# Token rows fetched by index and transposed, in place of gather products, in a four-layer mixture-of-experts step

## What is computed

```python
def moe(h, router_w, router_b, wg, wu, wd):
    x = h.reshape(B * T, D)                                   # 256 x 1024
    scores = jax.nn.sigmoid((x @ router_w).astype(jnp.float32))
    sel = scores + router_b.astype(jnp.float32)
    ...                                                       # best group of 4 experts, its best two
    w = w / w.sum(axis=-1, keepdims=True)
    combine = jnp.einsum('nk,nke->ne', w, jax.nn.one_hot(idx, N_EXPERTS, dtype=jnp.float32))
    hid = jax.nn.silu(jnp.einsum('nd,edf->nef', x, wg)) * jnp.einsum('nd,edf->nef', x, wu)
    y = jnp.einsum('nef,efd->nd', hid * combine[..., None].astype(hid.dtype), wd)
    return y.reshape(B, T, D)
```

## Time and profile before

| | |
|---|---|
| median of three runs | 1986.24 us (1983.18 to 1988.86) |
| the profiled execution | 1988.12 us, span 1986.3 us |
| TensorE busy (MATMUL records) | 1845.2 us, 93% |
| VectorE, ScalarE, GpSimd busy | 482.3, 385.8, 12.3 us |
| moved by DMA | 593.34 MB, mean 299 GB/s |
| granted TensorE clock, mean | 0.96 |

### The profile page before, as it was taken

The page is one execution under the profiler, slowest core; times in us unless marked ns, Lnnn a source line. Parts: engine busy times, 40 slices in busy tenths (PEclk is TensorE's granted clock), DMA queues, the critical chain, the costliest instruction groups (busy, mean ns, idle before and its releaser), DMA issues.

```text
span 1986.3 us, 22833 instructions
## 1 busy us (share of the span) xinstructions
PE 1845.2 (93%) x9280; PEld 1115.4 (56%) x9280; DVE 482.3 (24%) x1240; ACT 385.8 (19%) x801; POOL 12.3 (1%) x24
## 2 busy tenths in 40 slices
PE   4988999999999969999999997999999969999986
PEld 2656644545735858745445565844554748444543
DVE  0132511104300341411112434321112143311102
ACT  1132200003102660200002223200002142000002
POOL 1000000000000000000000000000000000000000
PEclk8998999999998988999999998999999989999988
DMA  9992599996997332579998884559999445599960
GB/s 328 350 401 80 212 397 427 428 419 242 356 359 259 117 122 91 215 311 428 428 427 311 321 292 170 215 216 425 428 429 401 140 193 211 233 424 429 427 265 22
DMA packets 126142, 593.34 MB, mean 299 GB/s; under 512 B 8008, under 2 KB 15312, under 8 KB 101088
## 3 DMA queue, kind: packets, MB, share of 16 engines
q1 hardware_dynamic: 115728, 585.12, 74.0%
q10 hardware_dynamic: 9840, 6.51, 1.1%
q0 software_dynamic: 480, 0.39, 0.1%
HBM read 587.28 MB, written 4.73 MB: 298 GB/s over the span
## 4 chain that ended last, share of the span: by engine, by line
PE 70%; DMA 18%; DVE 5%; ACT 4%; issue 2%; ACTq 1%; SPq 0%; DVEq 0%
PE PS L865 23%; PE PS L1358 18%; DMA ring<-in_moe_wu 16%; PE PS L1337 7%; PE PS L1369 7%; PE PS L894 3%; PE PS L914 2%; PE PS L1317 1%; DMA ring<-in_attn_w_qkv 1%; DMA ring<-in_w_mod 1%; PE PS L932 1%; ACT arena L594 1%; DVE RS L1495 1%; PE PS L1254 1%; PE PS L1322 1%
## 5 line engine op out<-in xcount | busy, mean ns | idle before, releaser
L1358 PE MATMUL PS<-ring,arena 128*64 128x512 f32 x1312 | 353.0, 595 | 4.8 <-DMA ring<-in_moe_wu 3.1
L1337 PE MATMUL PS<-arena 128*128 128x128 f32 (+3 forms) x1584 | 252.1, 317 | 10.8 <-ACT arena L800 4.4
L1337 PEld LDWEIGHTS PS<-arena 128*128 128x128 f32 (+1 forms) x1584 | 222.7, 195 | 52.5 <-issue 25.0
L800 ACT ACTIVATE arena<-PS 128x512 f32<-128x512 f32 (+2 forms) x131 | 71.3, 545 | 873.2 <-PE PS L1369 359.3
L865 PE MATMUL PS<-HS,ring 128*128 128x256 f32 x1024 | 233.8, 386 | 3.5 <-DVE HS L1565 1.6
L1369 PE MATMUL PS<-ring,arena 128*64 128x512 f32 x1024 | 226.8, 595 | 3.4 <-DVE arena L1822 3.4
L865 PEld LDWEIGHTS PS<-HS,ring 128*128 128x128 f32 x1024 | 194.8, 193 | 39.0 <-issue 10.0
L1358 PEld LDWEIGHTS PS<-ring,arena 128*64 128x64 f32 x1312 | 114.4, 137 | 159.6 <-issue 158.4
L1841 DVE TENSOR_TENSOR arena<-arena,PS 128x512 f32<-128x512 f32 x32 | 33.5, 1047 | 556.6 <-PE PS L1358 556.6
L865 PE MATMUL PS<-arena,ring 128*128 128x256 f32 (+1 forms) x672 | 147.6, 381 | 2.7 <-ACT arena L608 1.5
L1369 PEld LDWEIGHTS PS<-ring,arena 128*64 128x64 f32 x1024 | 70.7, 137 | 135.7 <-issue 127.9
(11 more groups left out here) (309 smaller groups left out, 1393.8 us busy)
## 6 DMA issues: line engine op xcount, KB each, us to landing
ring<-in_moe_wd SPq DMA_DIRECT2D x64, 2048.0 KB, 12.2
ring<-in_moe_wu SPq DMA_DIRECT2D x49, 2048.0 KB, 22.1
ring<-in_w_mod SPq DMA_DIRECT2D x48, 2048.0 KB, 16.1
ring<-in_moe_wg SPq DMA_DIRECT2D x33, 2048.0 KB, 19.7
arena<-in_moe_wg SPq DMA_DIRECT2D x32, 2048.0 KB, 20.8
HS<-in_moe_wu SPq DMA_DIRECT2D x16, 2048.0 KB, 28.4
ring<-in_mlstm_w_in SPq DMA_DIRECT2D x12, 2048.0 KB, 8.8
ring<-in_attn_w_qkv SPq DMA_DIRECT2D x6, 2048.0 KB, 20.1
```

The costliest lines, as they stand in the source:

```text
L800: A(dst, src, func).then_inc(S(sem), 1)
L1337: return mm(out, rows, onehot, start=first, stop=final, skip_group_check=True)
L1358: ins = mm(PS[64 * e:64 * e + 64, b, :], XG[:, k, 64 * e:64 * e + 64], w[:, k], start=(k == 0), stop=(k == KD - 1))
```

## The change

For pairs 1 to 7 the gather products are taken out. Token rows are written to memory once a layer, and for each pair GpSimd fetches the rows that its 128 slots need, by a list of 128 indices, into one of the two halves of `HT`; TensorE then turns them with eight transposes (`turn_x`). Pair 0 keeps its products. In detail:

- ScalarE, after each half of `HT` is copied, issues a DMA of it to `HR` in memory (2 x 512 KB).
- VectorE makes `OH`, for both halves of the tokens and pairs 1 to 7 at once: 1 where a token's rank is the slot (two comparisons of 128 x 896). `PB` is made for pair 0 alone, so later pairs have four comparisons in place of eight.
- TensorE's `slot_id`, between the two up groups of pair 0, multiplies each `OH` block by the token's number less 300 (one column): 14 products. VectorE adds 300 and turns the result into whole numbers, `IDX`. An unused slot gets 300, beyond the 256 rows; such an index is skipped and the slot keeps what it held (its weight is 0).
- GpSimd waits for `IDX`, for `HR` and for the half of `HT` to be free, and issues one indirect DMA a pair. Pair p's waits until pair p - 2 is turned (pairs 1 and 2: pair 0's gather).
- ScalarE's first SiLU waits for `slot_id`, since `OH` lies where `SG`, `HID` and `HTS` lie.
- SP, after the last weights of a layer, reads both halves of `HT` back from `HR` (2 x 512 KB), since the overflow step still gathers by products; ScalarE and VectorE wait for it before the next mixer, and TensorE before an overflow step.
- The many semaphores of the overflow step are folded into three. Its work is the same.

```diff
+        IDX = sb("IDX", [P, NPAIR], I32)
+        HR = nc.dram_tensor("token_rows", (N2, D), F32).ap()
+        OH = ar(4096, 2, NPAIR, 2, SLOTS)
...
                 n += 3 * NE
+                sp.wait_ge(S("gather"), 2 * NPAIR * (l + 1))
+                for s in range(2):
+                    sp.dma_start(HT[:, s], HR[P * s:P * s + P]).then_inc(S("back"), 16)
...
+            def rows(l):
+
+                pool.wait_ge(S("idx"), l + 1)
+                pool.wait_ge(S("rows"), 32 * (l + 1))
+                for p in range(1, NPAIR):
+                    pool.wait_ge(S("gather"), 2 * NPAIR * l + 2 * max(p - 1, 1))
+                    pool.indirect_dma_start(HT[:, p % 2], None, HR, bass.IndirectOffsetOnAxis(IDX[:, p:p + 1], 0),
+                                            bounds_check=N2 - 1, oob_is_err=False).then_inc(S(f"slot_rows{p % 2}"), 16)
...
                     run(A(rows, bank(b).rearrange("t (p k) -> t p k", k=KD), ACT.Copy), "ht_sb")
+                    if b % 2:
+                        load(HR[P * (b // 2):P * (b // 2) + P], HT[:, b // 2], "rows")
...
                     act.wait_ge(S("up"), 2 * n + 1)
+                    if first:
+                        act.wait_ge(S("slot_id"), l + 1)
                     evac(SG, bank(here[0]), ACT.Silu, "silu", n + 1)
...
+                def turn_x(banks, par, sem):
+
+                    for k in range(KD):
+                        ins = tp(bank(banks[k // 4], P * (k % 4), P * (k % 4) + P), HT[:, par, P * k:P * k + P], ident)
+                        if k in (3, 7):
+                            ins.then_inc(S(sem), 1)
+
+                def slot_id():
+
+                    pe.wait_ge(S("onehot"), 2 * (l + 1))
+                    for p in range(1, NPAIR):
+                        for s in range(2):
+                            ins = mm(bank(3, p, p + 1), OH[:, s, p].rearrange("t y n -> t (y n)"), c_("tid")[:, s:s + 1], start=(s == 0), stop=(s == 1))
+                    ins.then_inc(S("slot_id"), 1)
...
                         up(ws, here[g], "up", 2 * n + 2 if g == 0 else None)
+                        if first and g == 0:
+                            slot_id()
...
                     if more:
-                        pe.wait_ge(S("pw"), 8 * n + 16)
+                        pe.wait_ge(S("pw"), 4 * n + (4 * l + 12))
                         turn_w(here[1], "turn_w")
-                        gather(there, "gather")
+                        pe.wait_ge(S(f"slot_rows{1 - par}"), 8 * i + (48 * l + 8 if par else 64 * l + 16))
+                        turn_x(there, 1 - par, "gather")
...
                     wait(v, "turn_w", n)
-                    for j in range(8):
-                        slots(p + NPAIR * (j // 2 % 2), j % 2, j // 2 % 2, S1[:, 0:SLOTS], j >= 4).then_inc(S("pw"), 1)
-                    v.wait_ge(S("pw"), 8 * n + 8)
+                    for j in range(4):
+                        slots(p + NPAIR * (j // 2), j % 2, j // 2, S1[:, 0:SLOTS], True).then_inc(S("pw"), 1)
+                    v.wait_ge(S("pw"), 4 * n + (4 * l + 8))
+
+                def onehot(s):
+
+                    e = rk[:, s].rearrange("t (y p) -> t p y", y=2)[:, 1:NPAIR]
+                    at = S1[:, 0:SLOTS].unsqueeze(1).unsqueeze(1).broadcast_to([P, NPAIR - 1, 2, SLOTS])
+                    go(tt(OH[:, s, 1:NPAIR], at, last(e, SLOTS), ALU.is_equal), "onehot")
...
                 weights(1, n0 + 1)
+                onehot(0)
+                onehot(1)
...
+                v.wait_ge(S("slot_id"), l + 1)
+                idf = RT[:, 480:480 + NPAIR - 1]
+                go(ts(idf, bank(3, 1, NPAIR), 300.0, None, ALU.add))
+                go(v.tensor_copy(IDX[:, 1:NPAIR], idf), "idx")
```

More of the change, by code:

```diff
@@ L506, in _ @@
                 pool.dma_start(WA2[32 * d:32 * d + 16, :], I["gla2_w_a2"][d]).then_inc(S("load_a2"), 16)
+            rows(2)
+            rows(3)
         @block.scalar
@@ L806, in wts, with pair @@
                     evac(WTS[:, par, 0:N2], bank(b, 0, N2), ACT.Copy, "wts", n + 1)
-                def pair(n, par, more=True):
+                def pair(n, par, more=True, first=False):
                     here = BANKS[par]
                     act.wait_ge(S("up"), 2 * n + 1)
+                    if first:
+                        act.wait_ge(S("slot_id"), l + 1)
                     evac(SG, bank(here[0]), ACT.Silu, "silu", n + 1)
@@ L820, in moe @@
                 wts(n0, 0, 2)
-                pair(n0, 0)
+                pair(n0, 0, first=True)
                 pair(n0 + 1, 1)
@@ L842, in _ @@
                 affine(2 * l, l, 0)
+                wait(act, "back", 32 * l)
                 (lambda: attention(l // 3, l), mlstm, gla)[l % 3]()
@@ L848, in _ @@
             norm(2 * DEPTH)
+            act.wait_ge(S("back"), 32 * DEPTH)
             for k in range(KD):
@@ L1848, in moe @@
                 n0 = NPAIR * l
+                for j in range(4):
+                    slots(NPAIR * (j // 2), j % 2, j // 2, S1[:, 0:SLOTS], False).then_inc(S("pw"), 1)
+                v.wait_ge(S("pw"), 36 * l + 4)
                 weights(0, n0)
@@ L1906, in moe @@
-                        v.wait_ge(S("x_hid"), before + i)
-                        v.wait_ge(S("x_turn_h"), before + i)
-                        copy(HTS[:, :, 0:64], bank(6).rearrange("p (f t) -> p f t", f=4)[:, :, 0:64], "x_hts", before + i)
+                            ins = slots(e, j % 2, 0, S1[:, bass.ds(lo, SLOTS)], j >= 2).then_inc(S("x_v"), 1)
+                            v.wait_ge(S("x_v"), x_step(before, i, "x_p") + (j + 1))
+                        v.wait_ge(S("x_t"), x_step(before, i, "x_turn_w"))
@@ new lines, in moe @@
+                        copy(WTS[0:64, 0, 0:N2], PS[0:64, 5, 0:N2], "x_v", x_step(before, i, "x_wts"))
+                        v.wait_ge(S("x_t"), x_step(before, i, "x_gather"))
+                        for j, (sem, count) in enumerate((("x_v", x_step(before, i, "x_half")), ("x_v", x_step(before, i, "x_xg")))):
+                            copy(XG[:, 4 * j:4 * j + 4, 0:64], bank(6 + j).rearrange("p (k t) -> p k t", k=4)[:, :, 0:64], sem, count)
+                        v.wait_ge(S("x_t"), x_step(before, i, "x_up2"))
@@ L1909, in moe @@
+                        v.wait_ge(S("x_a"), x_step(before, i, "x_silu"))
+                        tt(by_k(HID[0:64]), row(SG[0:64]), row(PS[0:64, 5]), ALU.mult).then_inc(S("x_v"), 1)
+                        v.wait_ge(S("x_v"), x_step(before, i, "x_hid"))
+                        v.wait_ge(S("x_t"), x_step(before, i, "x_turn_h"))
+                        copy(HTS[:, :, 0:64], bank(6).rearrange("p (f t) -> p f t", f=4)[:, :, 0:64], "x_v", x_step(before, i, "x_hts"))
                 v.wait_ge(S("x_scatter"), before + nx)
@@ L1914, in _ @@
                 norm(2 * l, l, 0)
+                wait(v, "back", 32 * l)
                 (lambda: attention(l // 3, l), mlstm, gla)[l % 3]()
```

60 lines of the change are left out of this document (31 added, 29 removed).

## The result

| | before | after |
|---|---|---|
| median (4 runs each) | 1984.71 us (1981.3 to 1988.86) | 2010.06 us (2003.78 to 2014.8) |
| ratio, with its 95% interval | 1 | 1.0126 (1.0102 to 1.015) |
| the profiled execution | 1988.12 us, span 1986.3 | 2009.9 us, span 2008.1 |
| moved by DMA | 593.34 MB | 609.32 MB |
| granted TensorE clock, mean | 0.96 | 0.949 |

What follows compares the result with a forecast made beforehand. Prediction: DMA bounds the expert stages from the end of pair 0. Terms: 4 x (0.4 + 3.7) + 5.0 = +21.4 us, giving 2007.6 on the median; stated 2008, range 1991 to 2028.

Steps and rivals of the forecast that it cites:

- The bound: Expert stages: DMA sets the pace, 29.5 us a pair against TensorE's 28.63; TensorE savings in pairs 1 to 6 move nothing.
- One sign: Last pairs of the expert stage: time between two landings of `wu` grows from 29.5 to about 30.4 us.
- Pair 0: Pair 0 of each layer: `slot_id` +3.1, gather saving -2.7; on balance +0.4 us, from -2.0 to +0.6.
- Two of its own signs: Pair 0 stays within 1 us of before; layer 0's last `wu` lands 3 to 6 us later.
- VectorE and the first SiLU: Pair 0: one-hots ready near 228 us, before TensorE wants them at 230.4; SiLU done by 235.4, before 240.5.
- The first fetch: Pair 0: 8.2 us from index list to landing, taken as in time: 0, up to 4 us a layer.
- The bytes: Fetches 4 to 7, DMA-saturated part: rows take time from the weights, 3.7 us a layer, bounds 0 and 4.9.
- the even spread: Fetched rows spread evenly, 4 rows an engine: 0.61 us a fetch, 2.5 us a layer.
- the middle value: Fetched rows priced between even spreading (2.5) and a fullest engine moving 8 rows (4.9): 3.7 us a layer.
- The copies: Copy out near 217 us, in the idle part: 0; copy back's 2.5 us hidden before the next layer.
- The clock in the tail: Last up group: waits lower TensorE's clock in one or two layers, 3.3 us each; 5.0 in all, bounds 0 and 26.
- in every tail: Rival, 10%: the clock falls in each layer's tail, 6.5 us each instead of 5.0 in all; +21, 2029 us.

Runs made afterwards that it cites:

- experiment 1: Kernel before with eight transposes in place of the gather products of pairs 1 to 7, nothing else added: 1971.73 us, ratio 0.9952.
- experiment 2: Kernel before plus the one-hots, `slot_id` and the list of indices alone; gather products kept, nothing fetched: 2008.68 us, ratio 1.014.
- experiment 3: Kernel after with 64 columns in place of one in each `slot_id` product: 2003.12 us, ratio 1.0106.
- experiment 7: New order of SP's weight loads: on the kernel before 1970.7 us, ratio 0.9955; on the kernel after with 64-column `slot_id` 1992.25 us, ratio 1.0051.
- experiment 8: New weight order: kernel before with transposes alone, 1961.06 us; kernel after with 64-column `slot_id` and fetches that move nothing, 1971.64 us.
- experiment 4: Kernel after with 600 in place of 300 added to the indices, so fetches are issued but move no rows: 1998.7 us, ratio 1.0082.
- experiment 5: Kernel after with unused slots fetching row 0, so each fetch moves all 128 rows: 2017.76 us, ratio 1.0188.
- experiment 6: Kernel after without reading both halves of `HT` back from memory and without the waits for it: 2004.85 us, ratio 1.0129.
- e11: Kernel after with 64-column `slot_id`, the new order of weight loads and fetches that move no row: 1971.64 us, ratio 0.9934.

## Why the prediction was right, and where it wasn't

The forecast was 2008 us, within 1991 to 2028, with the change slower; measured were 2010.06. The sum was +21.4 us and the profiled span grew by 21.8, but its terms were off in both directions, by up to 9 us, so the agreement to 2 us is luck.

- **The bound.** Right. DMA share 1.01 at 428 GB/s from 260 to 431 us, as before, with TensorE's busy time in the same window down from 169.4 to 158.9 us. The saving on TensorE in pairs 1 to 6 was worthless: experiment 1 has it alone. One sign was read wrongly: the last pairs were to take 30.4 us, and the last two take 29.4, since the seventh fetch is issued at 361.24 and none falls into them; the three before take 30.1 to 30.6.
- **Pair 0.** The term that was mis-sized: +0.4 us a layer forecast, +2.7 measured (4.0 in layer 0, 2.3 in the others). The step that failed is the pricing of `slot_id` by the ranking products: that gave 3.1 us for the 14 products and nothing for what comes after them. They took 3.3 to 3.8, and the up group behind them 1.4 to 2.8 us more at half the clock. The prediction looked for clock falls only where TensorE waits; experiments 2 and 3 show one made by work. Two of its own signs failed with it: pair 0, which was to stay within 1 us of before, took 4.0 us more in layer 0, and the last `wu` landed 7.2 us later after the stage's begin, not 3 to 6.
- **VectorE and the first SiLU.** Right: the chain goes from the up group to `slot_id` and on with no wait for `OH` or for ScalarE.
- **The first fetch.** Right: the first fetch was issued at 233.67, and the two fetches issued in pair 0 landed 3.9 us later in the median; the turn began at 244.16. The margin was real only because DMA was idle: in experiments 7 and 8 it wasn't, and the margin was gone.
- **The bytes.** Forecast 14.8 us (3.7 a layer, the middle between rows spread evenly and rows crowded on one engine), measured 10.8, or 12.0 against the kernel whose fetches move nothing. Experiments 4 and 5 leave it between the even spread and the middle, experiment 8 puts it at the even spread. The Trainium skill, DMA: Bandwidth & Descriptors, section "The descriptor swizzle", would give an engine fixed groups of partitions and with it the middle value. The runs don't bear it out for these fetches: 3.0 us a layer for four of them in experiment 4, where the middle value is 3.7 and the even spread 2.5, and 4.0 for seven in experiment 8, where they are 6.4 and 4.3.
- **The copies.** Right. The copy back is experiment 6. The copy out has no run of its own, but the first fetch waited for `IDX` and not for it (the row of 233.67 below), and from the last ranking product to the first gather product it is 1.3 us both before and after.
- **The clock in the tail.** Forecast 5.0 us, in one or two layers at 3.3 each; measured 3.2, in two layers at 1.6 each. The number of layers was right by luck, since kernels with the same tail had none (experiment 6), one (experiment 3), two (experiment 5) and three (experiment 4). The price was half: it had been taken from a stretch of 13 us, and here the clock was down for only part of a group of 7 us. The rival "in every tail" came true in experiment 1 and not here. The Trainium skill, TensorE: Matmul & The Clock Gate, section "HAM oscillation — how this bites in real kernels", describes such a repetition; the runs agree that waits for DMA go ahead of such falls, here of 2.0 to 2.7 us ahead of the group, and show that it need not repeat: in experiment 6 three of four layers had a wait of 2.7 us there and no fall. What decides it stays open.

Terms against measurement: pair 0 +1.6 and +10.9; bytes +14.8 and +10.8; tails +5.0 and +3.2. The stage grew by 24.9 us, the rest of that one execution fell by 3, which is within what it moves by.

What stays open: why one execution has more clock falls in the tails than another, and whether `slot_id` placed where it doesn't delay pair 0 would bring the change to even.

## What to carry to other kernels

Before a saving on one engine is counted, find what ends the stage and how far the next bound lies behind it: here 75 us of saved products were worth 6 us of the stages where DMA set the pace, and 10 with the order in which TensorE did, because there the weights stand only 2.6 us behind it in 209. Rows that are fetched from memory compete with weights that stream at the full rate, nearly byte for byte; a product that makes them from what is in SBUF cost nothing here in the pairs in which TensorE wasn't the bound. An order of loads in which no free buffer waits behind an occupied one was worth 9 to 15 us here, with no change to the work.

## What the runs showed of the hardware

- *The clock can fall under a busy TensorE.* 28 records of one-column products ran without a gap, and in the kernel after the granted clock went from 1.00 to 0.50 2.5 to 3.1 us after they began, for 3.4 or 6.8 us; in five kernels it did so in every layer. With 64 columns it stayed at 1.00, in every layer of three kernels. The wide products were no slower: 3.27 us against 3.3 to 3.8.
- *An indirect fetch with 128 indices keeps GpSimd for 1.0 us*, and its landing depends on the queue much more than on its bytes. The GpSimd timeline of the kernel after, and the landings of its five fetches from 225 to 300 us:

```profile
233.67 1.07 POOL L521 DMA_INDIRECT arena<-token_rows,IDX  x1 [223.71 <-DVE IDX L1945]
235.04 1.01 POOL L521 DMA_INDIRECT arena<-token_rows,IDX  x1 [0.30 <-issue]
```

```profile
DMA to landing us min/median/max: 3.5/5.6/11.6
```

  The 3.5 us belong to an idle DMA system, the 11.6 to a full one. A fetch without a single row took 2.1 us in the idle one (experiment 4) and 8.30 in the full one (e11).
- *An index beyond the end moves nothing and costs nothing in the stream*: seven such fetches a layer left the stretch at 723.0 us against 724.2 without any.
